# Four blocks of modulation in place of two between the token tiles' transposes

## The chip, the cores and the metric

The program runs on one core of one Trainium2 chip. The metric is the time on the device of one whole execution, in microseconds (us). Everything is computed in float32: the large matrix products split each operand into a high and a low part (type fp32r) and add three products, high times high, high times low and low times high.

## What is computed

There are two blocks of a transformer, one after the other, on 256 tokens of width 1024. The first has two layers; each is four sublayers with a layer norm after each:

```python
for l in range(DEPTH):                                   # DEPTH = 2
    x = layer_norm(a * x + 0.5 * swiglu_ffn(x, ffn_w_in[l, 0], ffn_w_out[l, 0]), ...)
    x = layer_norm(a * x + mixer_sublayer(x, w_mix_in[l], ...), ...)
    x = layer_norm(a * x + memory_cross_attention(x, mem, ...), ...)
    x = layer_norm(a * x + 0.5 * swiglu_ffn(x, ffn_w_in[l, 1], ffn_w_out[l, 1]), ...)
```

The second block has two layers with attention and a feed-forward part each, for the 256 tokens and for a context of 256 more. Before each part its input is normed and modulated, and its output is gated, with vectors that come from a condition vector alone:

```python
def adaln(cond, mod_w, mod_b):
    return jnp.split(jax.nn.silu(cond) @ mod_w + mod_b, 6, axis=-1)   # six vectors of 1024

def modulate(h, shift, scale):
    return h * (1 + scale) + shift
```

These products, "the modulation" here, are 48 MB of weights for two rows of input. They depend on nothing that the first block computes, so they can be done at any time before the second block needs them.

## The kernel before

**One program, five engines.** `program` (L2803) is walked through once for each engine; each engine keeps the instructions that are its own. So the order in which the Python code runs is the order of each engine's queue, and a semaphore wait holds up all that is behind it on that engine.

**Weights.** Weights come in blocks of 512 KB (256 rows of 512 columns). SyncE loads them, in the order of use, into five `raw` slots. An ordinary block is then split: ScalarE writes its high part `whi` (a copy, "hi" below) and VectorE its low part `wlo` (raw minus high, "lo" below), into four slots each. `stage` (L462) writes out these three instructions for one block. `next_block` (L496), called where TensorE is about to use block u, stages up to block u + 3 (AHEAD = 3), and so decides where hi and lo of later blocks stand in the queues of ScalarE and VectorE. A raw slot is free for the next load when its block has been split, or, for a plain block, when TensorE has used it.

**Modulation.** Its blocks are plain: TensorE reads them from raw. The generator `modulation` (L959) does one block of 512 KB at each step, four of 96 steps make a group of 512 outputs. A group ends with a copy from PSUM to `modr` on ScalarE; some steps into the next group, `mod_columns` (L989) or `mod_rows` (L1003) add eight or two small matmul instructions and one on VectorE. Each step counts as 1.8 us where code goes by counted time. Steps are taken in `fill` (L371), which takes steps until the counted time is used up; in ten places of some of the feed-forward layers (`groups`, L1019); and in the second block, where `weave` (L417) takes one whenever neither of its two streams (the tokens' and the context's) has work that is due, where attention takes them, or where `modulated` (L1026) forces them because the next part needs the result.

**The seams.** A layer of the first block ends with `gemm_by_tile` (L564), which finishes the first tile of 128 tokens (t = 0) before the second (t = 1), so that the norm of the first runs beside the products of the second. It stages up to three blocks past its own last one (L595). `LayerNorm.steps` (L820) then does what stands between two layers: in its first part, TensorE transposes the first tile's normed y, and ScalarE scales and copies it to xh; in its second part TensorE transposes the second tile, VectorE writes the first tile's xl, and the second tile is scaled by VectorE and split into xh and xl. `between_layers` (L877) runs the first part, then the fill, then the second part. With `keep` it sets `co.keep`, so that the fill does not stage blocks, and the second part calls `stage_part` (L517) twice, each staging one ordinary block.

The lines that matter are these:

```python
if ahead and not (co.keep and u + 1 < co.staged):     # next_block, L506
    stage_to(co, u + AHEAD)

steps = norm.steps()                                  # between_layers, L880 on
if keep:
    next(steps)
co.keep = keep
fill(co, work, us)
end(steps)
```

There are five seams with modulation in them: after the first feed-forward part and after the cross attention of both layers, and between the first layer and the second.

Of the kernel before, what the change touches and what calls it, by code (L numbers as in the profile page):

```python
# [251 lines left out]
def alloc(co, name, shape, dt=F32):  # L252
    n = 4
    for s in shape[1:]:
        n *= s
    n = (n + 31) // 32 * 32
    assert co.base + n <= co.top, (name, co.base, n, co.top)
    i = co.names[name] = co.names.get(name, -1) + 1
    t = co.parts.sbuf(f"{name}{i}", shape, dt, co.base)
    co.base += n  # L260
    return t
# [24 lines left out]
def counts(co):  # L286

    return (pe_mark(co), co.s_dv.mark(), co.s_ac.mark(), co.s_po.mark(),
            tuple(s.mark() for s in co.s_par if s.n))
# [72 lines left out]
def flush(co):  # L362
    finish(co, *co.jobs)


def run(co, gen):
    for _ in gen:
        tick(co)


def fill(co, gen, us):  # L371

    while us > 0:
        took = next(gen, None)
        if took is None:
            return
        tick(co)
        us -= took
# [11 lines left out]
def end(gen):  # L390
    for _ in gen:
        pass
# [484 lines left out]
def between_layers(co, norm, work, us, keep):  # L877


    steps = norm.steps()  # L880
# [5 lines that stand above are left out]
    co.keep = False  # L886
# [280 lines left out]
def side_setup(co, fe):  # L1167

    A = co.A
    rows, bias, cs = alloc(co, "rows", [48, P]), alloc(co, "brows", [96, P]), alloc(co, "cs", [P, 16])  # L1170
    lng, lnb = alloc(co, "lngr", [64, P]), alloc(co, "lnbr", [64, P])
    e, rb, row = alloc(co, "bkt", [32, 512]), alloc(co, "rb", [32, 8]), alloc(co, "t5row", [8, 512])

    def gen():
        for _ in range(24):
            yield
        co.po.wait_ge(fe)
        d = (load_small(co, e[:, :], A["buckets"][:, :]), load_small(co, rb[:, :], A["rel_bias"][:, :]))
        yield from mod_setup(co, rows, bias, lng, lnb, cs, fe)
        b = next_bank(co)  # L1180
        co.pe.wait_ge(d, b.drained)
        t = co.pe.matmul(b.ap[0:8, :], rb[:, :], e[:, :], skip_group_check=True, start=True, stop=True).then_inc(co.s_pe)
        co.ac.wait_ge(t, fe)
        b.drained = a = co.ac.activation(row[:, :], b.ap[0:8, :], ACT.Copy).then_inc(co.s_ac)
        yield
        co.po.wait_ge(a)
        one = load_small(co, A["t5_one"], row[:, :])
        yield
        yield
        co.po.wait_ge(one)  # L1190
        src = A["t5_one"]
        src = bass.AP(tensor=src.tensor, offset=src.offset, ap=[[512, 8], [0, P], [1, 512]])
        co.t5 = load_small(co, A["t5"], src)
    return gen()
# [60 lines left out]
def rpb_scratch(co, z, fe):  # L1255

    A = co.A
    co.dv.wait_ge(fe)
    a = co.dv.memset(z[:, :], 0.0).then_inc(co.s_dv)
    yield  # L1260
    out = []
    co.po.wait_ge(a)
    for r in range(7):
        out.append(load_small(co, z[16 * r:16 * r + 16, 48:79], A["na_rpb_2"][0, :, r + 4, :]))
    yield
    yield
    yield
    co.po.wait_ge(tuple(out))
    one = load_small(co, A["na_one"].rearrange("r h w -> (r h) w"), z[:, :])
    yield  # L1270
    yield
    co.po.wait_ge(one)
    src, dst, done = A["na_one"], A["na"].rearrange("c r h w -> c (r h w)"), []
    for c in range(0, 64, 8):
        part = bass.AP(tensor=src.tensor, offset=src.offset, ap=[[0, 8], [1, 7 * 16 * P]])
        co.po.wait_ge(pe_mark(co))
        done.append(load_small(co, dst[c:c + 8, :], part))
        yield
        yield
        yield  # L1280
    co.nadep = tuple(done)


def ffn1(co, l, i, behind=None):

    A = co.A
    w = 0 if i == 0 else 1
    got = {}
    fe = counts(co)
    base = co.base  # L1290
    if behind is not None:
        spawn(co, behind)
    some = spawn(co, groups(co, 10), 6) if l != i else None
    norm = LayerNorm(co, co.y, got, 4e-5, (l, 3 * i), () if i == 0 else (1, 0))
    run(co, ffn(co, co.xt, A["ffn_w_in"][l, w], A["ffn_w_out"][l, w], residual(co, co.y, 2 * ALPHA, got, fe, 2, norm), ffn_tiles(co), True))
    if some in co.jobs:
        co.jobs.remove(some)
    co.base = base
    return norm
# [1474 lines left out]
def second(co, start):  # L2774
    A = co.A
    at = lambda off, name, shape, dt=F32: place(co, start + 1024 * off, name, shape, dt)
    small = lambda a, b, i: co.cst[:, a:b].rearrange("p (i n) -> p i n", i=i)
    co.passed, co.limit, co.top = set(), 24, TOP
    old, co.ch = co.ch, [co.cst[:, c:c + P].rearrange("p (k n) -> p k n", k=4) for c in (C_TRI, C_SM + 68)]
    co.ac.wait_ge(counts(co))  # L2780
    for a, b in zip(co.ch, old):
        co.chdep = co.ac.activation(a, b[:, :, :], ACT.Copy).then_inc(co.s_ac)
    tile = at(84, "ctx", [P, 2, D])
    co.po.wait_ge(counts(co))
    ready = load_small(co, tile[:, :, :], A["ctx_2"][0].rearrange("(t p) d -> p t d", p=P))
    co.stream = {1: Stream(tile, [ready, ready], small(C_SM, C_SM + 4, 2), counts(co))}
    co.sm, co.mx = small(C_SM + 4, C_SM + 12, 2), small(C_SM + 12, C_SM + 28, 4)
    co.smo, co.mxo = small(C_SM + 28, C_SM + 60, 2), small(C_SM + 60, C_SM + 68, 4)
    ev = Even(co, at(16, "kv", [P, 2, 4352]), at(50, "q", [P, 2560]), [at(60 + 4 * i, "etk", [P, 2, 512]) for i in range(2)],
              (at(68, "cqh", [P, 2, 256], F32R), at(70, "cql", [P, 2, 256], F32R)),  # L2790
              (at(72, "ckh", [P, 1, 256], F32R), at(73, "ckl", [P, 1, 256], F32R)),
              at(74, "ew", [P, 2, 512]), co.lb[:, :].rearrange("p (t n) -> p t n", t=2))
    weave(co, rows(co, at, ev), context(co, at, ev), 0.6)
    flush(co)
    for c in range(2):
        for t in range(2):
            co.sp.wait_ge(co.stream[0].ready[t][c])
            done = co.sp.dma_start(A["out"][t * P:(t + 1) * P, c * 512:(c + 1) * 512], co.x[:, t, c * 512:(c + 1) * 512]).then_inc(co.s_out, by=16)
    co.sp.wait_ge(done)
    co.sp.wait_ge([s.mark() for s in co.s_par if s.n])  # L2800


def program(co):  # L2803
    setup(co)
    start = co.base
    for l in range(2):
        co.base = start + 24576
        behind = even_setup(co, counts(co)) if l else side_setup(co, counts(co))
        co.base = start
        norm = ffn1(co, l, 0, behind)  # L2810
        flush(co)
        between_layers(co, norm, co.mods, 3.5, True)
        norm, kv = mixer(co, l)
        keys = kv.keys()
        between_layers(co, norm, keys, 5.5, False)
        run(co, keys)
        norm = cross(co, l, kv)
        between_layers(co, norm, co.mods, 3.5, True)
        co.base = start
        if l == 0:  # L2820
            co.base = start + 24576
            behind = rpb_scratch(co, alloc(co, "zero", [112, P]), counts(co))
            co.base = start
            norm = ffn1(co, 0, 1, behind)
            flush(co)
            between_layers(co, norm, co.mods, 3.5, True)
    second(co, start)


def first_and_second_block(nc, A, out):  # L2830
# [4 lines left out]
    with ExitStack() as ctx:  # L2835
        parts = Parts(nc, ctx)
        first = new_core(nc, A, parts, None)
        program(first)
        order = first.seen
        with nc.Block() as block:  # L2840

            @block.sync
            def _(e):
                program(new_core(nc, A, parts, order, "sp", e))

            @block.scalar
            def _(e):
                program(new_core(nc, A, parts, order, "ac", e))

            @block.gpsimd  # L2850
            def _(e):
                program(new_core(nc, A, parts, order, "po", e))

            @block.vector
            def _(e):
                program(new_core(nc, A, parts, order, "dv", e))

            @block.tensor
            def _(e):
                program(new_core(nc, A, parts, order, "pe", e))  # L2860
# [26 lines left out]
```

## Time and profile before

| | us |
|---|---|
| median of 3 runs | 2638.78 |
| lowest and highest | 2638.03, 2642.65 |
| the profiled execution, time | 2631.57 |
| its span, first to last instruction | 2629.8 |
| TensorE, matmul busy | 2541.4 (97%) |
| VectorE busy | 1689.3 (64%) |
| ScalarE busy | 1252.0 (48%) |
| mean granted TensorE clock, share of full speed | 0.992 |

The trace shows, for every instruction, its start, its length, and, where the engine was idle before it, for how long and which instruction of which engine ended that. PE is TensorE, DVE VectorE, ACT ScalarE, SPq the queue of SyncE that issues the transfers. Busy times of PE overlap a little, since a matmul starts before the one before it has ended.

### The profile page before, as it was taken

How to read it: one execution, taken by the hardware profiler on the slowest of the kernel's cores; microseconds unless marked ns; L12 is line 12 of the kernel's file. 1: busy time of each engine (PE TensorE's matmuls, PEld its weight loads, DVE VectorE, ACT ScalarE, POOL GpSimd, SP SyncE). 2: the span in 40 equal slices, each digit the busy share in tenths (PEclk: the TensorE clock that was granted, in tenths of full speed). 3: DMA queues.
4: the chain of work that ended last, by engine and by line, in shares of the span. 5: the costliest groups of instructions: out<-in, count | busy, mean ns of one | idle time of the engine just before them, and what ended most of it. 6: DMA issues, size and time to landing. Idle time of an engine off the chain costs nothing. (4 is left out here: it accounts for less than half of the span.)

```text
span 2629.8 us, 42228 instructions
## 1 busy us (share of the span) xinstructions
PE 2541.4 (97%) x16525; PEld 2195.0 (83%) x16525; DVE 1689.3 (64%) x2507; ACT 1252.0 (48%) x1798; POOL 170.4 (6%) x215
## 2 busy tenths in 40 slices
PE   8999999999999999999999998899999999999999
PEld 8998877889888888878798876687888888676998
DVE  5556686765475566766765667776565565756655
ACT  4445545544344445454554563465444444554443
POOL 1000000010011000000000200210000011110000
PEclk9999999999999999999999999999999999999999
DMA  7655455567566564456565535553456767635554
GB/s 236 219 187 161 137 187 173 192 201 266 189 224 209 192 225 134 157 169 207 176 201 184 165 98 162 192 175 104 160 157 228 232 205 198 191 117 182 173 186 137
DMA packets 276132, 479.25 MB, mean 182 GB/s; under 512 B 17616, under 2 KB 87320, under 8 KB 275872
## 3 DMA queue, kind: packets, MB, share of 16 engines
q1 hardware_dynamic: 265632, 445.24, 51.8%
q0 software_dynamic: 10304, 31.31, 4.0%
q8 instruction: 133, 2.18, 0.3%
q14 instruction: 63, 0.52, 0.1%
HBM read 475.33 MB, written 6.92 MB: 183 GB/s over the span
## 5 line engine op out<-in xcount | busy, mean ns | idle before, releaser
L126 DVE TENSOR_TENSOR wlo<-raw,whi 128x1024 fp32r<-128x1024 f32 (+3 forms) x786 | 911.3, 1172 | 686.3 <-ACT whi L167 611.0
L167 ACT ACTIVATE whi<-raw 128x1024 fp32r<-128x1024 f32 (+3 forms) x786 | 786.2, 1016 | 605.9 <-PE bank L175 427.2
L175 PE MATMUL bank<-xh,whi 128*128 128x256 f32 x2208 | 629.8, 285 | 6.9 <-DVE xl L126 5.4
L175 PE MATMUL bank<-xl,whi 128*128 128x256 f32 x2208 | 622.0, 282 | 0.0
L175 PE MATMUL bank<-xh,wlo 128*128 128x256 f32 x2208 | 621.7, 282 | 0.0
L175 PEld LDWEIGHTS bank<-xh,whi 128*128 128x128 f32 x2208 | 419.0, 190 | 23.4 <-issue 17.2
L175 PEld LDWEIGHTS bank<-xl,whi 128*128 128x128 f32 x2208 | 419.1, 190 | 1.1 <-issue 0.5
L175 PEld LDWEIGHTS bank<-xh,wlo 128*128 128x128 f32 x2208 | 418.8, 190 | 0.0
L175 PE MATMUL bank<-whi,xh 128*128 128x512 f32 (+2 forms) x632 | 255.0, 403 | 11.3 <-issue 5.3
L175 PE MATMUL bank<-whi,xl 128*128 128x512 f32 (+2 forms) x632 | 247.4, 391 | 0.0
L175 PE MATMUL bank<-wlo,xh 128*128 128x512 f32 (+2 forms) x632 | 246.8, 391 | 0.0
L175 PE MATMUL bank<-whi,uh 128*128 128x512 f32 x528 | 210.5, 399 | 2.1 <-DVE wlo L126 2.1
L175 PE MATMUL bank<-wlo,uh 128*128 128x512 f32 x528 | 208.5, 395 | 0.0
L175 PE MATMUL bank<-whi,ul 128*128 128x512 f32 x528 | 208.5, 395 | 0.0
L175 PEld LDWEIGHTS bank<-whi,xh 128*128 128x128 f32 x632 | 119.7, 189 | 51.9 <-issue 20.8
L175 PEld LDWEIGHTS bank<-whi,xl 128*128 128x128 f32 x632 | 119.8, 190 | 26.8
L175 PEld LDWEIGHTS bank<-wlo,xh 128*128 128x128 f32 x632 | 119.8, 190 | 25.6 <-issue 1.4
L175 PEld LDWEIGHTS bank<-whi,uh 128*128 128x128 f32 x528 | 99.0, 187 | 28.9 <-issue 6.3
L175 PEld LDWEIGHTS bank<-whi,ul 128*128 128x128 f32 x528 | 99.0, 187 | 24.1
L126 POOL TENSOR_TENSOR cst<-cst 128x8 f32<-128x8 f32 (+4 forms) x50 | 72.2, 1457 | 715.2 <-DVE cst L133 715.2
L175 PEld LDWEIGHTS bank<-wlo,uh 128*128 128x128 f32 x528 | 99.1, 188 | 22.5
L175 PE MATMUL bank<-ch,whi 128*128 128x256 f32 x352 | 101.2, 288 | 2.1 <-ACT whi L167 2.1
(432 smaller groups left out, 3849.3 us busy)
## 6 DMA issues: line engine op xcount, KB each, us to landing
raw<-in_ffn_w_in SPq DMA_DIRECT2D x280, 512.0 KB, 4.5
raw<-in_ffn_w_out SPq DMA_DIRECT2D x154, 512.0 KB, 4.7
raw<-in_w_mix_in SPq DMA_DIRECT2D x112, 512.0 KB, 3.5
raw<-in_mod_w SPq DMA_DIRECT2D x96, 512.0 KB, 4.8
raw<-in_od_w_in SPq DMA_DIRECT2D x40, 512.0 KB, 4.4
raw<-in_ffn_w_in SPq DMA_DIRECT2D x56, 256.0 KB, 2.9
raw<-in_w_branch SPq DMA_DIRECT2D x24, 512.0 KB, 3.5
raw<-in_ev_w_in SPq DMA_DIRECT2D x24, 512.0 KB, 3.9
```

The costliest lines, as they stand in the source:

```text
L126: return Made(self.e and self.e.tensor_tensor(out, a, b, op))
L167: return Made(self.e and self.e.activation(out, a, f, **k))
L175: return Made(self.e and self.e.matmul(out, lhs, rhs, **k))
```

## The change

At the five seams the counted time of the fill is 7 in place of 3.5. A step counts as 1.8, so that four steps are taken where two were. The seam between the mixer and the cross attention (its fill is the keys' product, 5.5) is as it was. The number of steps in all, 96, is the same.

```diff
@@ program
         norm = ffn1(co, l, 0, behind)
         flush(co)
-        between_layers(co, norm, co.mods, 3.5, True)
+        between_layers(co, norm, co.mods, 7, True)
         norm, kv = mixer(co, l)
         keys = kv.keys()
         between_layers(co, norm, keys, 5.5, False)
         run(co, keys)
         norm = cross(co, l, kv)
-        between_layers(co, norm, co.mods, 3.5, True)
+        between_layers(co, norm, co.mods, 7, True)
         co.base = start
         if l == 0:
...
             norm = ffn1(co, 0, 1, behind)
             flush(co)
-            between_layers(co, norm, co.mods, 3.5, True)
+            between_layers(co, norm, co.mods, 7, True)
```

## Rows read from the trace of the kernel before

**Rows 1.** Page, part 1: busy us (share of the span) x instructions.
```profile
PE 2541.4 (97%) x16525; PEld 2195.0 (83%) x16525; DVE 1689.3 (64%) x2507; ACT 1252.0 (48%) x1798; POOL 170.4 (6%) x215
```

**Rows 2.** Timeline of PE, first seam: start, length, engine, line, operation [idle before <-releaser].
```profile
203.84 1.07 PE L175 MATMUL bank<-raw,ch 128*32 128x256 f32 x16
206.81 1.09 PE L178 MATMUL bank<-cst,y 128*128 128x128 f32 x8 [1.90 <-DVE y L133]
209.09 0.36 PE L175 MATMUL bank<-xh,whi 128*128 128x256 f32 x1 [1.19 <-DVE xl L126]
...
212.47 0.35 PE L175 MATMUL bank<-xh,whi 128*128 128x256 f32 x1 [0.30 <-ACT whi L167]
```

**Rows 3.** Timeline of PE: the second tile's transposes at three other seams.
```profile
551.61 1.97 PE L178 MATMUL bank<-cst,y 128*128 128x128 f32 x8 [2.35 <-DVE y L133]
...
756.60 1.09 PE L178 MATMUL bank<-cst,y 128*128 128x128 f32 x8 [1.87 <-DVE y L133]
...
1303.89 1.09 PE L178 MATMUL bank<-cst,y 128*128 128x128 f32 x8 [1.23 <-DVE y L133]
```

**Rows 4.** Timeline of ACT, first seam.
```profile
207.03 0.60 ACT L167 ACTIVATE xh<-bank 128x512 fp32r<-128x512 f32 x1
...
208.34 1.05 ACT L167 ACTIVATE whi<-raw 128x1024 fp32r<-128x1024 f32 x1
```

**Rows 5.** Timeline of DVE, first seam.
```profile
202.22 1.22 DVE L126 TENSOR_TENSOR wlo<-raw,whi 128x1024 fp32r<-128x1024 f32 x1
...
205.94 0.81 DVE L133 TENSOR_SCALAR y<-y,mv,rs 128x1024 f32<-128x1024 f32 x1 [0.74 <-POOL rs L126]
206.67 0.68 DVE L126 TENSOR_TENSOR xl<-bank,xh 128x512 fp32r<-128x512 f32 x1
...
207.93 1.01 DVE L126 TENSOR_TENSOR xl<-bank,xh 128x512 fp32r<-128x512 f32 x2
```

**Rows 6.** Timeline of SyncE's queue, first seam: transfers issued.
```profile
204.54 16.71 SPq L123 DMA_DIRECT2D raw<-in_w_mix_in  x9
```

**Rows 7.** Page, part 6: transfers, KB each, median us from issue to landing.
```profile
raw<-in_w_mix_in SPq DMA_DIRECT2D x112, 512.0 KB, 3.5
raw<-in_mod_w SPq DMA_DIRECT2D x96, 512.0 KB, 4.8
```

**Rows 8.** Timeline of ACT, third seam: the copy that ends a group of modulation.
```profile
757.34 0.59 ACT L167 ACTIVATE modr<-bank 128x512 f32<-128x512 f32 x1
```

**Rows 9.** Windows: us, busy of PE, PEld, DVE, ACT, POOL, granted clock, DMA, GB/s.
```profile
202.00:214.00 12.00, 8.61 (x74) 7.18 (x73) 11.15 (x23) 8.86 (x17) 0.97 (x2) 1.00 0.44 148
555.00:557.00 2.00, 2.00 (x11) 2.00 (x11) 2.00 (x5) 1.11 (x3) 0.00 (x0) 0.50 0.00 0
557.00:559.00 2.00, 2.00 (x14) 2.00 (x13) 2.00 (x4) 1.44 (x2) 0.00 (x0) 0.69 0.33 107
```

**Rows 10.** Timeline of PE and a window, near the end of the span.
```profile
2433.84 0.47 PE L178 MATMUL bank<-cst,y 128*128 128x128 f32 x1 [4.52 <-DVE y L132]
...
2438.00:2440.00 2.00, 1.99 (x14) 1.62 (x12) 1.30 (x4) 0.63 (x1) 0.00 (x0) 0.75 0.00 0
```

**Rows 11.** Timeline of PE, second block, where the context stream needs the modulation.
```profile
1686.30 1.93 PE L175 MATMUL bank<-raw,cst 128*32 128x256 f32 x32
1688.82 1.02 PE L175 MATMUL bank<-modr,cst 128*2 128x512 f32 x2 [0.59 <-ACT modr L167]
1692.62 1.97 PE L178 MATMUL bank<-cst,etk 128*128 128x128 f32 x8 [2.78 <-DVE etk L126]
```

**Rows 12.** Timeline of PE, second block, the last steps of modulation.
```profile
2412.20 1.05 PE L175 MATMUL bank<-cst,modr 128*128 128x2 f32 x8
...
2416.36 1.02 PE L175 MATMUL bank<-modr,cst 128*2 128x512 f32 x2 [1.60 <-ACT modr L167]
2417.89 0.47 PE L175 MATMUL bank<-whi,xh 128*128 128x512 f32 x1 [0.51 <-DVE xl L126]
```

**Rows 13.** Windows, as rows 9: attention of the second block's last layer.
```profile
2345.00:2395.00 50.00, 50.00 (x431) 34.93 (x428) 29.70 (x67) 30.02 (x71) 2.19 (x4) 1.00 0.61 201
```

## The prediction

> **What bounds the kernel now.** I read the page's engine line first: TensorE is busy for 97% of the span, VectorE 64%, ScalarE 48% [rows 1]. So nearly every microsecond of TensorE's work is on the path, and what can be won is idle time of TensorE alone. I then read TensorE's timeline at the five seams that the change touches, in order of time. At the first one the two blocks of modulation run from 203.84 for 1.07 us; then TensorE is idle for 1.90 us until the second tile is normed (the releaser is DVE y), transposes it, and is idle again for 1.19 us until DVE has written xl [rows 2]. The other seams show the same first wait: 2.35, 1.87 (at 960.09 again, 1.88) and 1.23 us [rows 3]. Last I read ScalarE and VectorE there [rows 4, 5], since the wait before the first matmul of the next layer is ended by them.
>
> **What the change does, in steps.** A step of modulation counts as 1.8 us in fill. 3.5 lets two through, 7 lets four: 7, 5.2, 3.4, 1.6. Ten steps of the 96 therefore move from the second block to the five seams.
>
> **(1) The steps themselves at the seams: nothing.** Sixteen instructions, two steps, took 1.07 us [rows 2]; two more take about as much again, and once in a group the four small matmuls of mod_columns come with them (eight instructions, 1.05 us [rows 12]). The idle 1.90 covers 1.07, and nearly 2.1; the shortest, 1.23, still covers 1.07. If that cover were gone it would cost 1 us at a seam, but the second tile's transposes are not what comes last any more, by (2).
>
> **(2) Where the weight splits land in the queues: this is the cost.** While co.keep is set, next_block stages nothing as long as u + 1 < co.staged. gemm_by_tile leaves exactly three blocks staged past its last one (AHEAD = 3). Now these are modulation, modulation and the next layer's first weight block w1, and neither of two steps can reach the limit. Afterwards all three are modulation. The first and second step pass; at the third, u + 1 equals co.staged, and stage_to(u + 3) writes out three blocks at once: the fourth modulation block, w1 and w2. With them go hi(w1), hi(w2) on ScalarE and lo(w1), lo(w2) on VectorE, all ahead of the second tile's work, which between_layers writes only after fill. These queues run in order, so every scale, xh and xl of the second tile, and even the first tile's xl, waits behind them. In the kernel before lo(w1) stands at 202.22, under TensorE's last matmuls, and xl begins at 206.67, as soon as y is normed [rows 5].
>
> At the first seam afterwards: ScalarE is through with the first tile's xh at 207.63, as before [rows 4]. hi(w1) follows and takes 1.05 [rows 4]: 208.6. w2 needs the raw slot that the first modulation block holds until TensorE has used it; SyncE issues the transfer for such a slot at 204.54 [rows 6], and one takes 3.5 us [rows 7], so it lands at 208.1 and hi(w2) isn't held: 209.6. lo(w1) starts at 208.6 and two of them take 2 x 1.22, less the small overlap: lo(w2) ends at 210.9. xl of the first tile starts there instead of at 206.67: 4.2 us late. From xl to the first matmul the order of work is what it was (0.68, two scales, two xl [rows 5]), so the first matmul comes at 213.3 in place of 209.09. What else is late is covered: the copy of a full modulation group on ScalarE is 0.59 [rows 8] and falls behind hi(w2) at three seams, but ahead of hi(w1) at two (before the fourth feed-forward layer and before the second block, by the count of steps), where it adds some 0.45. Sum: 5 x 4.2 + 2 x 0.45 = 22 us. The bounds: 3.5 a seam if the splits overlap more (17.5), 5 if w2 lands a microsecond later under four transfers in a row (25).
>
> **(3) TensorE's clock.** At the seam with the longest wait now, 2.35 us, the granted clock is 0.50 in 555 to 557 and 0.69 in the next two microseconds, that is 1.2 GHz, and it comes back to full (2.4 GHz) after it; around the first seam, with waits of 1.90 and 1.19, it stays 1.00 [rows 9]. Another wait, of 4.52 us, is followed by 0.75 in 2438 to 2440 [rows 10]. The new waits before the first matmul are 1.19 + 4.2, or 5.4 us, longer than any of these, so I expect 1.2 GHz after each. What follows the 4.52 us is 5 us at that level (its end lies in the row of 0.75), half of it lost: 2.5. From this goes what the first block has spare, since the second block now waits 0.30 in any case [rows 2]. I take 1.9 at the three seams that are at full clock now, nothing new at the second, which pays already, and nothing certain at the last: 5.5 us; bounds 0 and 8.
>
> The Trainium skill ("TensorE: Matmul & The Clock Gate", section "HAM oscillation — how this bites in real kernels") prices such a stretch at half of its throttled time. Rows 10 would give by that rule 2.5 for a seam, 12.5 us for five if none of them paid now; the sum above does without it.
>
> **(4) What the second block gets back.** It has ten steps fewer. Ten times 0.53 are 5.3 us of TensorE's work. In the row of 1686.30 four forced steps stand together (1.93 us), then comes a wait of 0.59 for ScalarE's modr and its matmul, and then 2.78 of waiting for DVE's etk [rows 11]; ten steps earlier, the context stream need not take these steps before its feed-forward, whose matmuls could then fill the 2.78 too. Late in the second block a stretch of attention with 50.00 of 50 us busy [rows 13] loses three steps, and after it the last forced step and its wait of 1.60 for modr go away [rows 12], though xl is only 0.51 behind, so perhaps 1 us of the 1.60 comes back. Together 5.3 + 0.6 + 1 and some of the 2.78: I take 7.5. Bounds: 3, if TensorE only waits for DVE where the steps were; 12, if all waits named go.
>
> **Sum.** 22 + 5.5 - 7.5 = 20 us more. The profiled execution took 2631.57 (span 2629.8 and 1.8 around it), so it becomes 2651.6; the median of the shown runs is 7.2 higher, 2638.78, and becomes 2659.
>
> **Rivals.** (a) The change does what its name says: the idle time is filled, and the two splits cost nothing because ScalarE and VectorE have room (48 and 64% busy). Then (4) alone is left: 2638.8 - 7.5 = 2631. For it speaks that all five waits are there; against it that xl, behind lo(w2), is exactly what ends TensorE's second wait. It decides if the second tile's transposes come last instead. Chance 0.05.
> (b) The mechanism of (2) is right, but the second block's order of weaving changes (it goes by counted time, and five forced steps of 1.8 leave one stream) and gains up to 20 us there: about 2639. Nothing shows such a gain; chance 0.06.
> (c) Four modulation blocks pin four of the five raw slots, and the next layer's weights come too late as well. Now three weight blocks have landed or are on their way when the seam begins; afterwards w2 to w5 are issued together at 204.5 or later. At 3.5 us alone and 4.8 for the median modulation transfer [rows 7], w3 to w5 should land by 212, before TensorE wants them at 216. If not, 2 us more a seam: 2669. Chance 0.09.
> (d) The forecast: 2659, chance 0.80.
>
> **Range.** From the bounds, 17.5 + 0 - 12 = 5.5 to 25 + 8 - 3 = 30; 2645 to 2670 holds (d) and (c). Within 0.2% (5.3 us, about what a measurement of this kernel can tell from no change) I give 0.06, to faster 0.06, to slower 0.88.
>
> **What the profile should show.** (2) is right if at each seam DVE has two wlo directly before xl of the first tile, and TensorE's wait "DVE xl" before the first matmul has grown from 1.19 to some 5.4; wrong if it is under 2. (1) is right if the wait for DVE y shrinks by about 1. (3) shows as a granted clock under 1.00 just after the seams at 209, 759 and 962. (4) shows as no four steps together near 1686 and none after the attention near 2411, with the stretch from the last seam to the end shorter by 3 to 12 us. The prediction is wrong above all if the splits wait for nothing, or if the second block's gain is twice what I took.

## The result, and the profile after

| | before | after |
|---|---|---|
| median, us | 2639.32 (4 runs) | 2655.64 (4 runs) |
| lowest and highest | 2638.03, 2642.65 | 2653.80, 2656.82 |
| ratio | | 1.0063, 95% interval 1.0051 to 1.0075 |
| span of the profiled execution | 2629.8 | 2654.8 |
| mean granted TensorE clock | 0.992 | 0.986 |

The change makes the kernel 16.3 us slower; 20 were forecast, with 2645 to 2670 as the range. The engines' busy times are those of before, but for TensorE's, which is 8 us longer for the same number of instructions: by the clock record of the trace 77.0 us of this execution are at 1.2 GHz, against 41.0 in the profile of before. This is the page's part 1 of the kernel after, to be held against [rows 1]:

```profile
span 2654.8 us, 42229 instructions
PE 2549.8 (96%) x16525; PEld 2206.6 (83%) x16525; DVE 1689.4 (64%) x2507; ACT 1252.6 (47%) x1800; POOL 173.0 (7%) x215
```

The first seam on TensorE, answering [rows 2]:

```profile
204.44 1.93 PE L175 MATMUL bank<-raw,ch 128*32 128x256 f32 x32
207.13 1.09 PE L178 MATMUL bank<-cst,y 128*128 128x128 f32 x8 [0.76 <-DVE y L133]
213.94 0.55 PE L175 MATMUL bank<-xh,whi 128*128 128x256 f32 x1 [5.71 <-DVE xl L126]
```

In each row the first two numbers are start and length in us, and the bracket holds the idle time before it and what ended that. Four steps take 1.93 us, and the wait for y has shrunk from 1.90 to 0.76: that is what the change is after. But the wait for xl has grown from 1.19 to 5.71. Why xl is late stands in the queues of the other two engines, ACT first, then DVE, answering [rows 4, 5]:

```profile
207.62 0.60 ACT L167 ACTIVATE xh<-bank 128x512 fp32r<-128x512 f32 x1
208.11 1.99 ACT L167 ACTIVATE whi<-raw 128x1024 fp32r<-128x1024 f32 x2
210.00 0.59 ACT L167 ACTIVATE modr<-bank 128x512 f32<-128x512 f32 x1
212.90 0.38 ACT L167 ACTIVATE xh<-bank 128x256 fp32r<-128x256 f32 x1 [2.31 <-DVE bank L133]
```

```profile
206.26 0.81 DVE L133 TENSOR_SCALAR y<-y,mv,rs 128x1024 f32<-128x1024 f32 x1 [0.74 <-POOL rs L126]
209.26 2.36 DVE L126 TENSOR_TENSOR wlo<-raw,whi 128x1024 fp32r<-128x1024 f32 x2 [2.18 <-ACT whi L167]
211.54 0.68 DVE L126 TENSOR_TENSOR xl<-bank,xh 128x512 fp32r<-128x512 f32 x1
212.14 0.73 DVE L133 TENSOR_SCALAR bank<-bank,lncol 128x128 f32<-128x128 f32 x2
212.78 1.01 DVE L126 TENSOR_TENSOR xl<-bank,xh 128x512 fp32r<-128x512 f32 x2
```

VectorE has y at 207.07 and nothing but xl to do that anyone waits for. It idles for 2.18 us, because the next instruction in its queue is the low part of w1, whose high part stands behind ScalarE's last xh; then it makes two low parts; and then comes xl, at 211.54.

I read one measure off such rows at each seam: the time from the start of the first tile's transposes to the first matmul of the next layer. At the first seam they start at 202.88 before and 203.48 after, so it is 209.09 - 202.88 = 6.2 and 213.94 - 203.48 = 10.5. "Two blocks" is the time from that first matmul until two weight blocks (48 matmuls) have been started.

| us | seams 1 to 5 | sum | two blocks, seams 1 to 5 | sum |
|---|---|---|---|---|
| before | 6.2, 7.0, 6.2, 6.2, 6.8 | 32.3 | 6.3, 7.6, 6.3, 6.3, 7.1 | 33.5 |
| after | 10.5, 10.5, 11.0, 10.5, 11.0 | 53.5 | 8.1, 7.8, 7.2, 8.2, 7.2 | 38.4 |

The seams alone cost 21.2 us. Right after the first one TensorE is at the lower clock (windows, columns as in [rows 9]):

```profile
203.00:212.00 9.00, 4.47 (x51) 2.91 (x49) 5.30 (x8) 6.42 (x13) 0.55 (x1) 1.00 0.67 234
212.00:214.00 2.00, 0.06 (x1) 0.09 (x1) 2.00 (x6) 1.10 (x2) 0.00 (x0) 0.59 1.01 299
214.00:216.00 2.00, 2.00 (x10) 2.00 (x11) 2.00 (x7) 0.87 (x3) 0.00 (x0) 0.50 0.60 223
216.00:218.00 2.00, 2.00 (x11) 2.00 (x11) 2.00 (x4) 1.28 (x2) 0.00 (x0) 0.50 0.09 9
218.00:220.00 2.00, 2.00 (x14) 2.00 (x14) 0.90 (x1) 0.55 (x1) 1.57 (x2) 0.71 0.80 262
```

In the second block the forced steps of [rows 11] are gone. Where [rows 12] stood, TensorE has no step left, only the last group's small matmuls at 2438.53 and the transposes, and waits for xl:

```profile
2438.53 1.02 PE L175 MATMUL bank<-modr,cst 128*2 128x512 f32 x2
2439.48 1.09 PE L178 MATMUL bank<-cst,y 128*128 128x128 f32 x8
2442.84 0.48 PE L175 MATMUL bank<-whi,xh 128*128 128x512 f32 x1 [2.27 <-DVE xl L126]
```

### The profile page after: what moved, and what is told of

Same layout as the page of the kernel before. It is cut to its first block and busy times, and to the rows that moved or that the text cites. A ratio compares the mean times of both kernels' runs of the same rounds, so it can differ in the third digit from the quotient of the medians.

```text
span 2654.8 us, 42229 instructions
## 1 busy us (share of the span) xinstructions
PE 2549.8 (96%) x16525; PEld 2206.6 (83%) x16525; DVE 1689.4 (64%) x2507; ACT 1252.6 (47%) x1800; POOL 173.0 (7%) x215
## 3 DMA queue, kind: packets, MB, share of 16 engines
q8 instruction: 133, 2.18, 0.3%
## 5 line engine op out<-in xcount | busy, mean ns | idle before, releaser
L175 PE MATMUL bank<-x2h,whi 128*128 128x256 f32 x352 | 100.8, 286 | 3.0 <-issue 3.0
```

The source lines that it names most:

```text
L175: return Made(self.e and self.e.matmul(out, lhs, rhs, **k))
```

## The experiments

Each was timed beside the kernel before on the same chip, whose median there was 2639.1 in the first four and 2638.3 in the last four. Ratios are to that, with 95% intervals. The theory is that of the prediction: what is lost at a seam comes from weight splits that stand ahead of xl in two queues, not from the steps of modulation.

**b0_before: the kernel before once more.** No edit.

> The kernel before, unchanged, profiled on the same chip as the others. The profiled executions before and after stand 25 us apart, the medians 16. If the first profile of before was an unusually short execution, a second one has a span some 5 to 8 us longer, with its places shifted; if the profiling itself changes the time, it is again near 2630. Time against before: ratio 1.000.

Measured: 2638.4, ratio 0.9995 (0.9986 to 1.0004); the profiled execution has a span of 2637.9, 8.1 longer than the first profile of the same program. Its mean granted clock, the first profile's being 0.992:

```profile
core 0: 2637.9 us, clock 0.990
```

By the clock records of the two traces that is 54.6 us at 1.2 GHz, against 41.0. The seams are as before (32.1 in all), and in this execution the clock falls at the first one though the waits there are the same (1.89 and 1.19):

```profile
208.00:210.00 2.00, 0.81 (x9) 0.61 (x6) 2.00 (x6) 1.57 (x3) 0.00 (x0) 0.67 1.05 406
210.00:212.00 2.00, 2.00 (x9) 2.00 (x10) 2.00 (x7) 0.87 (x3) 0.00 (x0) 0.50 0.53 206
212.00:214.00 2.00, 2.00 (x12) 2.00 (x11) 2.00 (x4) 2.00 (x3) 0.00 (x0) 0.50 0.04 11
```

So the first profile of before was an execution with an unusually full clock: its time, 2631.57, is below all 43 others timed of this kernel beside the experiments (2634.69 to 2644.08), whose median clock is 0.990. Up to 6.8 us of the 8.1 are half of the 13.6 us more at 1.2 GHz; what makes up the rest is open. By place, 4.4 of the 8.1 lie behind the first matmul after the last seam, 2.6 in the two blocks after the first four seams. The comparison of spans that fits the medians is this one with after: 2654.8 - 2637.9 = 16.9, or 16.8 before rounding.

**e1_four_split_early: the four steps without the late splits.**

```diff
 # gemm_by_tile, t == 0
-            stage_to(co, blocks[-1][2] + AHEAD)
+            stage_to(co, blocks[-1][2] + AHEAD + (2 if w.tensor.name in (co.A["ffn_w_out"].tensor.name, co.A["xa_wo"].tensor.name) else 0))
```

with the counted time 7 of the changed kernel. Now five blocks past the last are staged under its products: four of modulation and w1. u + 1 stays below co.staged for all four steps. TensorE's, SyncE's and GpSimd's instructions are those of the changed kernel, one for one; only ScalarE and VectorE have another order.

> Four blocks of modulation at the seams as after, but the split of the next layer's first weight block stays where it was before (three blocks of modulation and one more staged under the last product, so that nothing is staged within the fill). TensorE's and SyncE's orders are those of after. Theory (the place of the splits in the queues): xl is on time at every seam, the wait before the first matmul is 1.2 again, the clock stays full after the seams 1, 3 and 4, and the sum is before plus what the second block does, by the profile of after between -7 and +3 us, so 2632 to 2642. Rival (four steps at a seam are themselves too long, or pin the raw slots): stays at 2650 to 2656.

Measured: 2633.3, ratio 0.9977 (0.9967 to 0.9988). The seams are 6.2, 6.8, 8.9, 6.2, 6.8. The first one, on PE and then DVE:

```profile
204.58 1.93 PE L175 MATMUL bank<-raw,ch 128*32 128x256 f32 x32
207.54 1.09 PE L178 MATMUL bank<-cst,y 128*128 128x128 f32 x8 [1.03 <-DVE y L133]
209.81 0.36 PE L175 MATMUL bank<-xh,whi 128*128 128x256 f32 x1 [1.19 <-DVE xl L126]
```

```profile
206.67 0.81 DVE L133 TENSOR_SCALAR y<-y,mv,rs 128x1024 f32<-128x1024 f32 x1 [0.74 <-POOL rs L126]
207.40 0.68 DVE L126 TENSOR_TENSOR xl<-bank,xh 128x512 fp32r<-128x512 f32 x1
```

With the same TensorE order and the same four raw slots held, the seam is whole again. The rivals that the steps are too long or pin the slots fall, at four seams of five. The seams are still 2.7 longer in all than in b0_before (34.9 against 32.1), so they aren't what makes this version faster than the kernel before. What differs too is the clock: its median over 7 executions is 0.992, against 0.990 in those of the kernel before, and the two blocks after the seams take 32.3 in all, against 33.5 and 36.8 in the two profiles of before. How the gain divides between the clock and the second block isn't shown. At the third seam something else shows:

```profile
751.53 1.93 PE L175 MATMUL bank<-raw,ch 128*32 128x256 f32 x32
755.85 1.05 PE L175 MATMUL bank<-cst,modr 128*128 128x2 f32 x8 [2.39 <-ACT modr L167]
```

There the first of the four steps ends a group. Its copy to modr stands behind ScalarE's scales of the first tile and is ready at 755.8; the small matmuls that come two steps later wait for it, and the second tile's transposes stand behind them.

**e2_two_splits_late: the late splits without the steps.** Two steps, and

```diff
-            stage_to(co, blocks[-1][2] + AHEAD)
+            stage_to(co, blocks[-1][2] + AHEAD - (1 if w.tensor.name in (co.A["ffn_w_out"].tensor.name, co.A["xa_wo"].tensor.name) else 0))
...
     fill(co, work, us)
+    if keep:
+        stage_part(co)
+        stage_part(co)
     end(steps)
```

(and next_block stages nothing under co.keep).

> Two blocks of modulation as before, in the same places of TensorE's order, but the splits of the next layer's first two weight blocks are written out after the fill, ahead of the second tile's scales and the first tile's xl, as they stand after. Theory: all of the seams' loss comes though no step is moved: 4 to 5 us a seam with the clock's part, so 2639 + 20 to 26 = 2659 to 2665, and the wait for xl 5 to 6 us. Rival (the two added steps cost): no change, 2639.

Measured: 2663.7, ratio 1.0088 (1.0075 to 1.0102). The seams are 10.5, 11.0, 11.0, 10.9, 11.0, 54.4 in all. DVE at the first:

```profile
209.74 2.36 DVE L126 TENSOR_TENSOR wlo<-raw,whi 128x1024 fp32r<-128x1024 f32 x2 [2.19 <-ACT whi L167]
212.01 0.68 DVE L126 TENSOR_TENSOR xl<-bank,xh 128x512 fp32r<-128x512 f32 x1
```

The same wait and the same two low parts as in the changed kernel, with TensorE's instructions in the order of the kernel before. The loads of the two blocks are late too, but nothing waits for them: ScalarE makes both high parts from 208.59 on, right behind its last xh (208.09, 0.60 long). So the queues' order is enough for the whole loss of the seams. The waits for xl are 5.7 to 6.6, a little above the 5 to 6 expected. The changed kernel is 8 us better than this one in the medians and 7.5 in the spans: 4.8 of these lie behind the last seam, 0.9 in the seams, the others elsewhere in the first block.

**e3_three_steps: at which step the splits come in.** Counted time 5.3 at the five seams.

> Three steps of modulation at each seam (counted time 5.3). Theory: the threshold lies between two and three, since the third step finds only three blocks staged; it stages not two but three weight blocks ahead of xl, the third landing last. So the loss is as large as with four steps or larger by about 1 us a seam: 2655 to 2662, wait for xl 6 to 7 us. Rival (the loss grows with the steps): half of it, about 2647, wait for xl about 3.5.

Measured: 2670.3, ratio 1.0115 (1.0101 to 1.0129), worse than expected. Three steps are worse than four. The seams are 11.6, 11.7, 11.6, 12.1, 12.1:

```profile
208.30 3.49 DVE L126 TENSOR_TENSOR wlo<-raw,whi 128x1024 fp32r<-128x1024 f32 x3 [2.19 <-ACT whi L167]
211.71 0.68 DVE L126 TENSOR_TENSOR xl<-bank,xh 128x512 fp32r<-128x512 f32 x1
```

As stage_to(u + 3) is reached by the third step in either kernel, with three steps all three blocks it writes out are weights; with four, one of them is modulation. The seams' 59.2 are 5.7 above those after, as expected. What I left out is the second block: the stretch from the last seam to the end is 1327.5 here, 1322.6 after and 1328.0 in b0_before. This looks as if almost nothing came back with half of the steps moved, but it isn't shown: in the first profile of before that stretch is 1323.6, so one execution of each can't tell. By the clock records 47 us of it are at 1.2 GHz here, 46 after and 39 in b0_before.

**e7_one_split_late: the price by number.** As e2 with one stage_part.

> Two steps as before, and only the first weight block's split is written out after the fill. None costs 6.2 us from the first tile's transposes to the first matmul, two 10.5 to 11, three 11.6 to 12.1. Theory: the first late split costs most, since VectorE waits for the high part behind ScalarE's scales (3.1), and each more 1.2 for its low part: 9.3 to 9.5 here, and 2639 + 5 x 3.2 + 2 to 5 = 2657 to 2660. Rival (the same for each split, 1.5 to 2.1): 8.0.

Measured: 2655.3, ratio 1.0062 (1.0048 to 1.0076); seams 9.3, 9.9, 9.8, 9.8, 9.9. At the first seam none, one, two and three late splits give 6.2, 9.3, 10.5 and 11.6: the first costs 3.1, and each more 1.1 to 1.2, the length of one low part. The time came out 2 us below what was expected; the first seam is as expected, the others are 0.3 to 0.4 above the 9.3 to 9.5.

**e6_low_parts_late: which queue.** As e2, but SyncE's loads and ScalarE's high parts of w1 and w2 stay under the last product, and only VectorE's low parts come after the fill.

> Two steps as before. The high parts of the next two weight blocks are made early, under the last product; only their low parts, on VectorE, stand ahead of xl. Theory: VectorE alone is then delayed by two low parts, 2.4 us, counted from the end of the norm: from the first tile's transposes to the first matmul 8.5 to 8.6 instead of 6.2 (10.5 to 11 with both engines' parts late). With the clock's part 5 x 3 = 15: 2654. Rival (the delay is ScalarE's place alone): 6.2, no change.

Measured: 2648.9, ratio 1.0040 (1.0025 to 1.0055); seams 8.2, 7.8, 8.2, 8.2, 7.9.

```profile
205.26 0.81 DVE L133 TENSOR_SCALAR y<-y,mv,rs 128x1024 f32<-128x1024 f32 x1 [0.74 <-POOL rs L126]
205.99 2.35 DVE L126 TENSOR_TENSOR wlo<-raw,whi 128x1024 fp32r<-128x1024 f32 x2
208.26 0.68 DVE L126 TENSOR_TENSOR xl<-bank,xh 128x512 fp32r<-128x512 f32 x1
```

The wait of 2.19 for whi is gone, the 2.35 are left. So a seam's loss with two late splits, 4.3 at the first, is 2.2 of waiting for ScalarE's place and 2.35 of low parts, less 0.3, since the second tile's norm begins earlier when no low part stands ahead of it. The total is 5 us under what was expected, because the seams lose 8.1 together instead of 12 and the clock's part is smaller too (two blocks: 38.9, against 36.8 in b0_before).

**e5_matmuls_in_wait: the clock's share.** The changed kernel with

```diff
         second = [(k0, nk) + self.turn(1, k0, nk) for k0, nk in ((0, 2), (2, 2), (4, 4))]
+        if co.keep:
+            idle = next_bank(co)
+            co.pe.wait_ge(idle.drained)
+            for _ in range(4):
+                idle.drained = co.pe.matmul(idle.ap, co.cst[:, C_ID:C_ID + P], co.cst[:, 0:512], start=True, stop=True, skip_group_check=True).then_inc(co.s_pe)
```

> The changed kernel with four matmuls more at each seam (float32, 128x512, into a bank that nobody reads, about 1.0 us each), put on TensorE between the second tile's transposes and the wait for xl, which is 5.4 to 5.9 long. Their results are not used. Theory (part of the seams' loss is TensorE's clock after the wait): the first matmul comes as late as in the changed kernel, 10.5 to 11 after the first tile's transposes, but the next two blocks take 6.3 to 6.6 instead of 7.2 to 8.2; five times 1.2 to 1.4, so 2655.6 - 6 to 7 = 2649. Rival (the clock falls for another reason, or the lost half is covered by waits for splits): 2655.

Measured: 2652.6, ratio 1.0054 (1.0041 to 1.0067), 2 to 3 us better than the changed kernel (1.0063) where 6 to 7 were expected. First seam, then the two windows after it:

```profile
207.53 3.60 PE L175 MATMUL bank<-cst 128*128 128x512 f32 x8
213.41 0.36 PE L175 MATMUL bank<-xh,whi 128*128 128x256 f32 x1 [2.28 <-DVE xl L126]
```

```profile
212.00:214.00 2.00, 0.59 (x5) 0.62 (x6) 2.00 (x7) 1.38 (x3) 0.00 (x0) 1.00 1.00 334
214.00:216.00 2.00, 2.00 (x19) 2.00 (x18) 2.00 (x5) 1.11 (x3) 0.00 (x0) 1.00 0.35 135
```

At four seams the first matmul is as late as in the changed kernel and the clock stays at 1.00. Two blocks take 6.3, 6.3, 6.1, 6.3, 6.3: 31.3 in place of 38.4. So it is the idle time that lowers the clock, and it costs up to 7 us in five seams. The third seam is another matter. There the clock falls right after the wait of 2.38 for modr, before the added matmuls begin, and they take 5.63 us in place of 3.60:

```profile
764.28 1.54 PE L175 MATMUL bank<-cst,modr 128*128 128x2 f32 x8 [2.38 <-ACT modr L167]
765.68 1.95 PE L178 MATMUL bank<-cst,y 128*128 128x128 f32 x8
767.42 5.63 PE L175 MATMUL bank<-cst 128*128 128x512 f32 x8
```

```profile
766.00:768.00 2.00, 2.00 (x9) 1.76 (x8) 2.00 (x4) 0.12 (x1) 0.07 (x1) 0.50 1.13 361
```

So they end after xl is there, and the seam is 13.5 in place of 11.0, which gives back 2.5. The intervals of the two ratios overlap, so the size of the net gain is not settled.

**e4_three_at_third: can the version of e1 be bettered.** As e1, with three steps and four blocks staged ahead at the third seam.

> The version with four steps and no split ahead of xl, but with three steps at the third seam (between the layers). There the four steps cost 2.65 us in its profile, since the group's copy to modr is behind ScalarE's scales and the small matmuls two steps later wait for it, with the second tile's transposes behind them. Theory: with three steps these matmuls fall after the seam, the stretch from the first tile's transposes to the first matmul is 6.2 there as at the first seam instead of 8.85, and the time is 2633 - 2.5 = 2631. Rival (such a wait is made up for by later work): the same 2633.

Measured: 2632.9, ratio 0.9978 (0.9969 to 0.9987). The third seam is whole:

```profile
749.48 1.50 PE L175 MATMUL bank<-raw,ch 128*32 128x256 f32 x24
752.43 1.09 PE L178 MATMUL bank<-cst,y 128*128 128x128 f32 x8 [1.45 <-DVE y L133]
754.71 0.36 PE L175 MATMUL bank<-xh,whi 128*128 128x256 f32 x1 [1.19 <-DVE xl L126]
```

All five seams are those of before (32.3), but the median is that of e1 within the interval, so that the 2.65 us can't be shown in the time. Runs of one kernel here spread by 10 us (2626.8 to 2636.6). Either version is 0.2% faster than the kernel before, and 0.8% faster than the changed one.

## Why the prediction was right, point by point

The sum of the prediction was 22 + 5.5 - 7.5 = 20. Against b0_before, whose time and clock are those of a usual execution, the difference of the profiled spans, 16.8, parts like this: seams 21.3 (53.5 - 32.1), the two blocks after the first four seams +2.2, from the first matmul after the last seam to the end -5.3, and the rest of the first block, taken as what is left, -1.4.

- **(1) The steps themselves cost nothing: right at four seams.** The wait for y went from 1.90 to 0.76 at the first. At the third it was wrong: the wait of 2.38 for modr was not foreseen. I had counted the small matmuls' 1.05 but not that they wait for a copy that ScalarE makes behind its scales. In the changed kernel it was hidden by the late xl, as the prediction says of anything that delays the transposes; e1 shows it bare, 2.65 us.
- **(2) The splits: right, 22 forecast, 21.3 measured**, with the instructions in the order that was read from the code, w2 landing in time, and the shift at the first seam 4.2 forecast (10.5 - 6.2 = 4.3 measured). e1 removes it alone, e2 makes it alone. That copies to modr stand ahead of hi(w1) at the third and fifth seam and add 0.45 there was right (11.0 against 10.5). By seam the loss against the first profile is 4.3, 3.5, 4.8, 4.3 and 4.2, where 4.2, 4.2, 4.65, 4.2 and 4.65 were forecast: the second and fifth were longer than the others before the change (7.0 and 6.8), which the forecast of one loss for all leaves out. Rival (a) falls with the wait of 5.71, rival (c) with e1, which holds the same four slots.
- **(3) The clock: the direction right, the size mis-sized.** Against the first profile two blocks took 4.9 longer in all, near the 5.5. But that profile had full clock at seams where other executions of the same kernel haven't: in b0_before the two blocks after the first and third seam take 8.2 and 7.3, where the first profile has 6.3. Against b0_before it is 1.6 for five seams. The step that failed is "three seams that are at full clock now": it rested on a single execution. The 1.9 for a seam that does go from full to half clock fits (1.8 at the first), though the working gives 2.5 - 0.30 = 2.2, and three times 1.9 are 5.7 and not 5.5. The whole price of the clock after the changed kernel's seams is some 7 (38.4 against 31.3 in e5), of which the kernel before pays 2.2 in one profile and 5.5 in the other. The rule of the Trainium skill ("TensorE: Matmul & The Clock Gate", section "HAM oscillation — how this bites in real kernels"), half of the throttled time, gives 2.5 for a stretch of 5 us, an estimate. The rows show 1.8 for the first seam (8.1 against 6.3), less than by the rule; 0.30 of the rest is the wait before the second block that is there anyway [rows 2].
- **(4) The second block: the direction right, 7.5 too high.** From the first matmul after the last seam to the end it is 5.3 less than in b0_before, but only 0.9 less than in the first profile. The two profiles of the kernel before have 1323.6 and 1328.0 there, and those of the three programs with all ten steps moved 1322.6, 1323.1 and 1321.4 (after, e1, e5). The means are 3.4 apart, just over the lower bound of 3, and no pair is more than 6.6 apart. The forced steps near 1686 and 2411 are gone as described. The last group's modr,cst matmuls are still there. In place of the waits of 1.60 for modr and 0.51 for xl stands one of 2.27 for xl, so none of the 1.60 came back, where I had taken 1. Rival (b), a gain of 20 there, didn't come.
- **The base, and what was luck.** The time forecast, 2659, is 3.4 above the measured one. Against b0_before, with the two blocks of all five seams in the clock's part (so that 4.7 is left of the 5.3 behind the last seam), the parts measured are 21.3 + 1.6 - 4.7 - 1.4 = 16.8, for 22 + 5.5 - 7.5 = 20. The clock was priced 3.9 too high and the seams 0.7, and 1.4 were won elsewhere in the first block, which the sum doesn't have; the second block's return was 2.8 too high, which works the other way. So the total is closer than its smaller terms, and that is luck. The profiled execution was forecast at 2651.6 and took 2656.53, since it was counted from the first profile.

Open is what makes up at least 1.3 of the 8.1 us between the two profiles of the kernel before, how much the second block gets back in a usual execution, and whether the wait for modr at the third seam is worth anything in the time.

## What to carry to other kernels

When work is added in a gap, look at what its code writes out besides itself: here a third step crossed a prefetch limit and put two weight splits ahead of the instruction that the gap was waiting for, and VectorE, which the gap was waiting for, had no room in that place (11.15 of 12 us busy [rows 9], though 64% over the whole span). Move the prefetch's limit with the amount of work (one edit of a count turned +0.6% into -0.2%). And compare a profile with several of the other kernel, not with one: one profiled execution can stand 8 us beside the next of the same program.

## What the runs showed of the hardware that I had not expected

TensorE's granted clock after a short wait differs between executions of the same program: after waits of 1.90 and 1.19 us it stays 1.00 in one profile, and is 0.50 right after them in another, after waits of 1.89 and 1.19. After the waits of 5.4 to 5.9 it was 0.50 at each of the four seams that had one; with 3.60 us of matmuls put into the first of them, of which 2.28 were left, it stayed 1.00, as at the other three. At the third seam of that run (e5) it fell after a wait of 2.38; in the changed kernel the wait of 2.38 is there too, and it fell only in the wait of 3.75 that follows.
